# Adding an expert's rows to the tokens: a 0/1 selection with gated rows in two rounded parts, in place of a gated selection with 32-bit rows

## The reference

```python
def moe_ffn(h, w_router, b_router, w1, b1, w2, b2):
    ...
    logits = (hf @ w_router + b_router).astype(jnp.float32)
    top_v, top_e = lax.top_k(logits, TOP_K)
    gates = jax.nn.softmax(top_v, axis=-1)
    ...
    def expert_block(args):
        xi, e = args
        hc = xi @ w1[e] + b1[e]
        g, u = hc[:, :D_EXPERT], hc[:, D_EXPERT:]
        g = jnp.minimum(g, SWIGLU_LIMIT)
        u = jnp.clip(u, -SWIGLU_LIMIT, SWIGLU_LIMIT)
        hm = (u + 1.0) * (g * jax.nn.sigmoid(SWIGLU_ALPHA * g))
        return hm @ w2[e] + b2[e]

    yb = lax.map(expert_block, (xb, block_e)).reshape(P, D)
    y = jax.ops.segment_sum(yb.astype(jnp.float32) * gate_buf[:, None], tok_buf, num_segments=T)
```

## Time and profile before

| what | value |
|---|---|
| median of 3 runs | 1804.92 us (1804.87 to 1807.25) |
| profiled execution, span of its instructions | 1801.1 us |
| PE matmuls busy | 1732.4 us, 96% |
| DVE busy | 958.6 us, 53% |
| ACT busy | 528.5 us, 29% |
| POOL busy | 841.8 us, 47% |
| DMA | 560.95 MB, mean 311 GB/s |

### The profile page before, as it was taken

One profiled execution on the slowest core, in us unless ns is written; L12 is line 12 of the kernel. 1 busy time (PEld: TensorE's weight loads), 2 busy tenths in 40 slices (PEclk: granted clock), 3 DMA queues, 4 the chain that ended last, 5 costly groups with the idle time before them and its releaser, 6 DMA issues.

```text
span 1801.1 us, 29517 instructions
## 1 busy us (share of the span) xinstructions
PE 1732.4 (96%) x10968; PEld 1099.2 (61%) x10969; DVE 958.6 (53%) x1438; ACT 528.5 (29%) x830; POOL 841.8 (47%) x492
## 2 busy tenths in 40 slices
PE   8999998998999999999999999999999999999997
PEld 8999996888899988888433333333333333333332
DVE  7777664566777766856543343343444434334334
ACT  6444444555644454463110110110101011011011
POOL 0000011000000038664577777777777767777774
PEclk9999999999999999999999999999999999999999
DMA  9877543234486634337999999999999999999994
GB/s 382 272 257 270 196 166 115 89 115 183 166 279 223 212 128 162 132 134 300 374 430 428 429 428 429 429 428 429 428 429 429 428 384 428 429 428 429 429 429 202
DMA packets 55261, 560.95 MB, mean 311 GB/s; under 512 B 6208, under 2 KB 7360, under 8 KB 14400
## 3 DMA queue, kind: packets, MB, share of 16 engines
q1 hardware_dynamic: 54912, 560.03, 77.7%
q10 hardware_dynamic: 288, 0.07, 0.0%
HBM read 559.03 MB, written 1.05 MB: 311 GB/s over the span
## 4 chain that ended last, share of the span: by engine, by line
PE 66%; DMA 16%; DVE 5%; ACT 5%; issue 4%; POOL 3%; SPq 0%; POOLq 0%; DVEq 0%; ACTq 0%
PE bank L1354 16%; DMA stage<-w_exp_in 15%; PE bank L731 11%; PE bank L733 10%; PE bank L732 10%; PE bank L1443 8%; POOL ring L1928 3%; PE bank L1366 2%; PE bank L1332 2%; ACT w_hi L1503 1%; DVE bank L1953 1%; DMA ring<-stream 1%; PE bank L1344 1%; ACT arena L1866 1%; PE bank L858 1%
## 5 line engine op out<-in xcount | busy, mean ns | idle before, releaser
L1928 POOL COPY ring<-stage 128x2048 f32<-128x2048 f32 x372 | 694.6, 1897 | 250.6 <-DMA stage<-w_exp_in 101.5
L1354 PE MATMUL bank<-ring,arena 128*64 128x512 f32 x2112 | 475.4, 596 | 15.6 <-POOL ring L1928 15.1
L731 PE MATMUL bank<-x_hi,w_hi 128*128 128x256 f32 (+1 forms) x1336 | 384.4, 288 | 19.2 <-DVE x_lo L1953 5.4
L733 PE MATMUL bank<-x_hi,w_lo 128*128 128x256 f32 (+1 forms) x1336 | 379.6, 284 | 0.0
L732 PE MATMUL bank<-x_lo,w_hi 128*128 128x256 f32 (+1 forms) x1336 | 379.2, 284 | 0.0
L1354 PEld LDWEIGHTS bank<-ring,arena 128*64 128x64 f32 x2112 | 141.7, 136 | 313.4 <-issue 233.1
L1908 POOL TENSOR_TENSOR w_lo<-ring,w_hi 128x512 fp32r<-128x512 f32 x104 | 135.2, 1334 | 393.2 <-ACT w_hi L1503 393.2
L731 PEld LDWEIGHTS bank<-x_hi,w_hi 128*128 128x128 f32 x1336 | 252.6, 189 | 27.3 <-issue 13.1
L733 PEld LDWEIGHTS bank<-x_hi,w_lo 128*128 128x128 f32 x1336 | 252.9, 189 | 0.0
L732 PEld LDWEIGHTS bank<-x_lo,w_hi 128*128 128x128 f32 x1336 | 252.1, 189 | 0.2
L1503 ACT ACTIVATE w_hi<-ring 128x2048 fp32r<-128x2048 f32 (+1 forms) x123 | 224.4, 1825 | 91.5 <-PE bank L731 86.9
(11 more groups left out here) (381 smaller groups left out, 1986.4 us busy)
## 6 DMA issues: line engine op xcount, KB each, us to landing
stage<-w_exp_in SPq DMA_DIRECT2D x124, 2048.0 KB, 10.5
stage<-w_exp_out SPq DMA_DIRECT2D x62, 2048.0 KB, 10.5
ring<-stream SPq DMA_DIRECT2D x119, 1024.0 KB, 4.9
arena<-ada SPq DMA_DIRECT2D x48, 512.0 KB, 4.4
ring<-w_exp_in SPq DMA_DIRECT2D x8, 1024.0 KB, 9.0
ring<-w_exp_out SPq DMA_DIRECT2D x4, 1024.0 KB, 14.1
cst<-const_in SPq DMA_DIRECT2D x1, 1608.0 KB, 20.6
arena<-b_exp SPq DMA_DIRECT2D x3, 384.0 KB, 8.2
```

Of the source, the lines that this page charges most:

```text
L731: begin = mm(out_, wh, xh, start=start, stop=False)
L733: return begin, mm(out_, wl, xh, start=False, stop=stop)
L1354: last = mm(bank[2 + gu][pr, :], xT[:, k % 4, k // 4, :], ring[:, k, c0:c0 + 512], start=False, stop=(k == KD - 1), tile_position=pos)
L1928: nc.gpsimd.tensor_copy(ring[:, j, :], stage[:, 2 * PAIR_PLACE[j // 2 % 3] + j % 2, :]).then_inc(in_place, 1)
```

## The change

`SG` still holds the selection times the gate, and it is still transposed. DVE now reads the transposed product from `bank[0]` twice: it sums each row over the 256 tokens, which gives the row's gate (`row_gate`, since a row belongs to one token), and it compares each element with zero, which gives a 0/1 `ST` of the rounded 32-bit type that PE takes in one pass. ACT no longer copies `ST`. When the second matrix is done, ACT multiplies by the gate as it copies the rows to `ye_hi` (rounded), and DVE writes what the rounding left, `ye_lo`. `back_to_tokens` does two one-pass products for each two-pass product of before, with `ye_hi` and with `ye_lo`. PE waits for DVE's `m_yl` where it waited for ACT's `m_ys`, in the loop and after it. Ahead of the loop one more tile is set to zero. Six semaphores of the block table become two that are counted up; the operations there are the same. The constants lie in a place that is named by hand, with `ye_lo` in a part of them that is no longer used.

```diff
         gate = sm_area.take(2, E)
+        row_gate = sm_area.take(1)
...
-        ST = a.take(2, P)
+        a.at += -a.at % 8
+        ST, _ = at_place("ST", [P, 2 * P], f32r, over=arena_at + a.at * 4)
+        a.take(2 * P)
...
-        ye = a.take(512)
+        a.at += -a.at % 8
+        ye_hi, _ = at_place("ye_hi", [P, 512], f32r, over=arena_at + a.at * 4)
+        a.take(512)
+        ye_lo, _ = at_place("ye_lo", [P, 512], f32r, over=cst_at + -(-(dead + 3 * 512) // 8) * 32)
...
             def back_to_tokens(r, banks=(6, 7)):
 
                 for mp in range(2):
+                    mt = 2 * r + mp
                     for j, _, pr in halves:
-                        mt = 2 * r + mp
-                        last = mm(bank[banks[j]][:, mp * 256:mp * 256 + 256], ye[pr, mt * P:mt * P + P],
-                                  ST[pr, :, :].rearrange("p a b -> p (a b)"),
-                                  start=True, stop=True, tile_position=(64 * j, 0))
+                        to = bank[banks[j]][:, mp * 256:mp * 256 + 256]
+                        mm(to, ye_hi[pr, mt * P:mt * P + P], ST[pr, :], start=True, stop=False,
+                           tile_position=(64 * j, 0))
+                    for j, _, pr in halves:
+                        to = bank[banks[j]][:, mp * 256:mp * 256 + 256]
+                        last = mm(to, ye_lo[pr, mt * P:mt * P + P], ST[pr, :], start=False, stop=True,
+                                  tile_position=(64 * j, 0))
                 last.then_inc(m_comb, 1)
...
                 first(e, range(0, 4))
-                pe.wait_ge(m_ys, g + 1)
+                pe.wait_ge(m_yl, g + 1)
                 pe.wait_ge(m_sts, g + 1)
...
-                act.wait_ge(m_xt, g + 2)
-                act.wait_ge(m_comb, g * 2 + 2)
-                A(ST[:, :, :].rearrange("p a b -> p (a b)"), bank[0][:, 0:256], ACT.Copy).then_inc(m_sts, 1)
+                act.wait_ge(m_sts, g + 2)
                 act.wait_ge(m_y, g + 1)
-                A(ye, bank[5][:, :], ACT.Copy).then_inc(m_ys, 1)
+                A(ye_hi[:, :], bank[5][:, :], ACT.Copy, scale=row_gate).then_inc(m_ys, 1)
...
-            mark(V.memset(ye, 0.0))
-            mark(V.memset(ST, 0.0))
+            mark(V.memset(ye_hi[:, :].bitcast(f32), 0.0))
+            mark(V.memset(ye_lo[:, :].bitcast(f32), 0.0))
+            mark(V.memset(ST[:, :].bitcast(f32), 0.0))
...
                 V.tensor_copy(xT[:, :, :, :].rearrange("p a b c -> p (a b c)"), bank[1][:, :]).then_inc(m_xts, 1)
+                V.reduce_sum(row_gate, bank[0][:, 0:256], AX.X)
+                ts(ST[:, :], bank[0][:, 0:256], 0.0, None, ALU.is_gt).then_inc(m_sts, 1)
+                dve.wait_ge(m_ys, g + 1)
+                stt(ye_lo[:, :], bank[5][:, :], row_gate, ye_hi[:, :].bitcast(f32), ALU.mult, ALU.subtract)\
+                    .then_inc(m_yl, 1)
```

More of the change, by code:

```diff
@@ L553, in build @@
         numbered = sem("numbered")
[L554 to L559, removed]
+        table_part = sem("table_part_from_dve")
+        KEYS, PLACED, PAST = 1, 2, 3
+        table_sum = sem("table_sum_from_pe")
+        RANKS, CUMULATED, TABLES = 1, 2, 3
         m_S = sem("m_S")
@@ L575, in build @@
         m_y = sem("m_y")
-        m_ys = sem("m_ys")
+        m_ys = sem("m_y_high")
+        m_yl = sem("m_y_lower")
         m_comb = sem("m_comb")
@@ L1374, in _ @@
             gather_part(0, bank[7])
-            pe.wait_ge(keys_ready, 1)
+            pe.wait_ge(table_part, KEYS)
             mm(bank[1][0:E, 0:1], before_it[0:E, :], const("ones", 0, 1, E), start=True, stop=True)\
-                .then_inc(rank_ready, 1)
+                .then_inc(table_sum, 1)
             gather_part(1, bank[7]).then_inc(m_gath, 1)
             keep_running(2, bank[2])
-            pe.wait_ge(placed, 1)
+            pe.wait_ge(table_part, PLACED)
             mm(bank[6][0:E, 0:1], up_to[0:E, :], nb_col[0:E, :], start=True, stop=False, **kw)
             mm(bank[6][0:E, 1:2], at_rank[0:E, :], neg_nb[0:E, :], start=False, stop=True, **kw)\
-                .then_inc(cum_ready, 1)
-            pe.wait_ge(past_ready, 1)
+                .then_inc(table_sum, 1)
+            pe.wait_ge(table_part, PAST)
             width = MAX_BLOCKS + 1
@@ L1393, in _ @@
             mm(bank[0][0:1, order_at:order_at + E], expert_col[0:E, :], at_rank[0:E, :],
-               start=False, stop=True, **kw).then_inc(table_sums, 1)
+               start=False, stop=True, **kw).then_inc(table_sum, 1)
             pe.wait_ge(m_xg, 1)
@@ L1447, in _ @@
                 last.then_inc(m_y, 1)
-            pe.wait_ge(m_ys, n_blocks + 1)
+            pe.wait_ge(m_yl, n_blocks + 1)
             pe.wait_ge(m_sts, n_blocks + 1)
@@ L2505, in _ @@
             settle()
-            ts(at_rank[0:E, :], const("iota", 0, E, E), rank_col[0:E, :], None, ALU.is_equal).then_inc(placed, 1)
-            dve.wait_ge(cum_ready, 1)
+            ts(at_rank[0:E, :], const("iota", 0, E, E), rank_col[0:E, :], None, ALU.is_equal).then_inc(table_part, 1)
+            dve.wait_ge(table_sum, CUMULATED)
             link(V.tensor_copy(cum_nb[0:E, :], bank[6][0:E, 0:2]))
             ts(past[0:E, :], const("iota", 0, MAX_BLOCKS + 1, E), cum_nb[0:E, 0:1], None, ALU.is_ge)\
-                .then_inc(past_ready, 1)
+                .then_inc(table_part, 1)
             def where(g):
@@ L2542, in _ @@
             width = MAX_BLOCKS + 1
-            dve.wait_ge(table_sums, 1)
+            dve.wait_ge(table_sum, TABLES)
             mark(ts(block_i[:, :], bank[0][0:1, 0:2 * width], float(E - 1), None, ALU.min))
@@ L2549, in _ @@
             mark(V.tensor_copy(order_i[:, :], bank[0][0:1, order_at:order_at + E]))
-            mark(V.memset(ye, 0.0))
-            mark(V.memset(ST, 0.0))
+            mark(V.memset(ye_hi[:, :].bitcast(f32), 0.0))
+            mark(V.memset(ye_lo[:, :].bitcast(f32), 0.0))
+            mark(V.memset(ST[:, :].bitcast(f32), 0.0))
             settle()
             dve.sem_inc(order_ready, 1)
-            dve.sem_inc(m_ys, 1)
+            dve.sem_inc(m_yl, 1)
             dve.sem_inc(m_sts, 1)
```

7 lines of the change are left out of this document (4 added, 3 removed).

## The result

| | before | after |
|---|---|---|
| median | 1805.49 us | 1809.89 us |
| ratio, 95% interval | | 1.0025 [1.0019, 1.0031] |
| span of the profiled execution | 1801.1 us | 1807.9 us |

The change makes the kernel 0.25% slower, 4.4 us by the medians: more than the 2.0 us forecast, more than the 0.2% that a measurement of this kernel can tell from no change, and beyond the end of the range. The two profiled executions are 6.8 us apart. That of before was a lucky one: about 2.0 us lie around a span in every run, so it took some 1803.1 us by that estimate, while the fastest of the 20 timed runs here took 1803.82.

What follows compares the result with a forecast made beforehand. The DMA's weight transfers, with four pauses and PE's tail, were taken to set the end. Pauses at 888 (+2.2), 1462 (-0.4), 1480 (+0.2) and tail (0) gave +2.0 on 1804.92: 1806.9 us, range 1802.5 to 1809.0.

Steps and rivals of the forecast that it cites:

- What bounds the kernel: Whole expert stage: its end is the transfers' fixed time, plus DMA pauses, plus PE's work after the last weights.
- the four pauses: DMA with nowhere to write: about 4.1 us near 868, 1.4 near 888, 3.0 near 1462, 1.4 near 1479.
- Rival 4: Expert stage: PE is the bound after all and all 26 us of its saving count, 1779 us; chance 0.03.
- `back_to_tokens` at 0.67: PE, each call: eight rounded passes overlap in pairs, 0.67 us instead of 1.06, saving 0.4 each, 0.8 a block.
- Rival 2: PE: rounded pairs do not overlap, `back_to_tokens` is not shortened, only the tail grows by 0.75, 1805.7 us; chance 0.18.
- The additional memset comes ahead of DVE's first block and falls into a wait for POOL: DVE ahead of the loop: the memset is hidden, `select` ending with POOL's third copy even if begun 0.5 us later.
- The pause at 888, +2.2: First block: an earlier POOL copy catches DVE's operations, PE waits about 3 us, the transfer of 887.64 comes 2.2 later.
- The pauses at 1462 and 1480, -0.4 and +0.2: Around the block without weights: first transfer 0.4 us earlier; PE then waits 1.0 for DVE, second transfer 0.2 later.
- Rival 3: Block without weights: three operations caught, PE waits 2.9 us, pause at 1480 grows another 1.9, 1808.8 us; chance 0.14.
- The tail, 0: Program's end: 0.75 us more for `ye_lo`, less 0.4 for each of two `back_to_tokens`, together about 0.
- Hidden edits: DVE's sum and comparison (1.3 us at most) hide behind PE's second matrix; memset and merged semaphores cost nothing.
- The range: Total time: 1802.5 to 1809.0 us, taking in the first three rivals and leaving the fourth out.

Runs made afterwards that it cites:

- pe_alone: Kernel before with rounded `ye` and `ST` and each product done twice with the same rows, lower part left out; ratio 0.9999 to the kernel before, 1804.52 us.
- before_memset512: Kernel before with one more memset, 128x512 of an unused tile (0.48 us), between those of `ye` and `ST`; ratio 1.0029 to the kernel before.
- after_memset_early: Kernel after with only the memset of `ye_lo` moved ahead of DVE's wait for the block tables; ratio 0.9999 to the kernel before.
- head_first: Kernel after with `ye_lo` computed in the next block, between `SG` and `onehot2`, and a memset of one column; ratio 1.0011 to the kernel before.
- dve_alone: Kernel after with PE's four products of two passes; `ye_lo` computed and waited for but not added; ratio 1.0025 to the kernel before.

## Why the prediction was wrong, step by step

- **What bounds the kernel**, the four pauses and the end: right. The block table shows it: 0.8 us a block is won in the stretch that PE paces, 5.6 us in seven blocks, and is gone by block 11. `pe_alone` has PE's whole gain and a ratio of 0.9999. Rival 4 is out with it.
- **`back_to_tokens` at 0.67:** right, 871.97 to the next start at 872.64. Rival 2 (the pairs don't overlap) is out.
- **The failed step: "The additional memset comes ahead of DVE's first block and falls into a wait for POOL".** I followed the 0.5 us only as far as `select`, which did wait for POOL's third copy in the earlier trace rows and could take it. Between the memset and `select` stand the two scalings, and they had only 0.56 us from their start to POOL's first copy, 0.17 from their end. I looked at DVE's rows around POOL's fourth copy and never at those around its first. The term was set at nothing; `before_memset512` measures it at 5.4 us by the second block and 0.29% in all, and in the kernel after it makes 4.2 of the 4.65 (4.65 less the 0.45 that are left when the memset is moved).
- **The pause at 888, +2.2:** the mechanism is there, the size is not. `pe_alone` and the early memset put it at +0.40 and +0.45, because DVE waits for three copies there and not for four: I had the fourth follow the third at once, and it waited 0.26 and 0.46 us for its transfer. With the memset in place the pause grows by 4.65: PE's wait of 3.74 and the 1.5 that the gathering loses at half clock, less the 0.6 that the two `back_to_tokens` save, are 4.6 of it. The fall of the clock stood nowhere in the prediction.
- **The pauses at 1462 and 1480, -0.4 and +0.2:** right. The transfers that end them come 0.4 earlier and 0.3 later by their issues, and PE's wait is 1.01 (forecast 1.0); blocks 21 to 32 give 0.27 back (forecast 0.2). Rival 3 (one more copy there) did not come.
- **The tail, 0:** of its three terms two lie behind the start of the last L1453, +0.75 and -0.4; measured there are +0.94 (PE's wait for `ye_lo`, 1.72 against 0.78) and -0.4, and 0.5 more for the clock: 1.05 and not 0.35.
- **Hidden edits:** the sum and the comparison are hidden. `ye_lo` is not held by the copies in any block, as taken from the earlier trace rows: its 33 times lie between 750 and 753 ns. In the profile's groups (busy, mean ns) it has

```profile
L1961 DVE SCALAR_TENSOR_TENSOR ye_lo<-bank,small,ye_hi 128x512 fp32r<-128x512 f32 x33 | 24.8, 751 | 219.0 <-ACT ye_hi L1882 219.0
```

- **The range** ended at 1809.0, since none of my rivals was about the operations ahead of the loop. Rival 3, slower, came nearest to the measured time, with 1808.8, by a mechanism that did not occur. It is luck, too, that the forecast had the right sign: its +2.0 rests on the +2.2, which is 0.4 without the memset.

The sum mended by the runs: +0.45 and -0.3 for the pauses, -0.4 for the last `back_to_tokens(1)` in the loop, +0.6 for the end and 0.5 to 1.35 for its clock, together 0.9 to 1.7 us, of which the times of `after_memset_early` allow 1.4 at most; and 4.2 us for the memset's place.

## What to carry to other kernels

A short operation put into a busy engine's setup costs nothing or several microseconds, depending on what it pushes: follow it to the next operation that meets another engine's copies, and compare its length with the margin there, in the trace. Then try it in another place before you judge the rest of a change: here the same memset, a few operations earlier, turned 0.25% slower into no change. The gain of 0.8 us a block on an engine that doesn't set the end was worth nothing here, and it moved the times at which other engines meet.

## What the runs showed of the hardware

- **POOL's copy holds DVE for whole copies, and the loss is a step.** Two 128x32 operations took 0.39 us when they began 0.49 us or more ahead of the copy, and 3.77 to 3.78 when they began 0.01 to 0.03 ahead. The Trainium skill (SBUF — State Buffer, the section "Who interferes with whom") has one engine hold the ports for a whole instruction; two holds of 1.89, a copy each, agree with it. It goes the other way too: in `pe_alone` the second operation of `SG` began 0.05 us ahead of a copy and took 0.30, and that copy took 2.00; in `after_memset_early` one that began 0.05 ahead took 2.00, and the copy 1.90. So a lead of 0.05 by the profile's starts can fall either way. Operations that read PSUM (`ye_lo`, 0.75) were not held.
- **PE's granted clock fell after some waits and not after others.** After waits of 3.64 to 3.74 us in the first block it was 0.57 to 0.60 in the following 4 us, and the gathering took 2.9 to 3.6 us instead of 1.94; after 1.1 to 1.2 us it stayed at 1.00, and so it did after the 3.33 us of `head_first`. At the program's end it fell to 0.50 after two waits of 1.72 and 1.87 us with 16 short products between them; unused products in the waits kept it at 1.00. In `dve_alone` it stayed at 1.00 there too, after waits of 1.71 and 1.49 us with products of 2.00 us between them. What tells these cases apart is open.
- **One part of sixteen can stay late for hundreds of microseconds.** In after the last part of each weight transfer came 1.2 us later from 950.4 us on, up to the pause near 1468, while the DMA moved 428 GB/s as in before. The lateness begins with the first landing behind a 16 KB packet of instructions (1.02 us) in ten of eleven profiles; no experiment was aimed at it.
